# Product-key experts on one core: the order of the row gathers, top-k two heads ahead, and the sample on 128 partitions

## The reference

```
qry   = (h @ w_query) as 8 heads x 2 halves x 128
half  = qry . sub_keys                  # 8 heads x 2 halves x 128 scores
half_s, half_i = top_k(half, 16)        # per half
cand  = half_s[0] (+) half_s[1]         # 16 x 16 sums
best_s, best_j = top_k(cand, 16)        # 16 experts of a head
idx   = half_i[0] * 128 + half_i[1]     # at best_j
g     = softmax(best_s)
act   = gelu(h . expert_u[idx])         # 16 dot products per head
out  += (g * act) . expert_v[idx]       # 16 weighted rows per head
```

## Time and profile before

| | us |
|---|---|
| median of 3 runs (lowest, highest) | 1561.77 (1561.24, 1566.16) |
| span of the profiled execution | 1514.1 |

### The profile page before, as it was taken

The page is one execution under the profiler, slowest core; times in us unless marked ns, Lnnn a source line. Parts: engine busy times, 40 slices in busy tenths (PEclk is TensorE's granted clock), DMA queues, the critical chain, the costliest instruction groups (busy, mean ns, idle before and its releaser), DMA issues.

```text
span 1514.1 us, 12192 instructions
## 1 busy us (share of the span) xinstructions
PE 1087.7 (72%) x2877; PEld 468.7 (31%) x2877; DVE 807.6 (53%) x1626; ACT 204.8 (14%) x580; POOL 602.9 (40%) x586
## 2 busy tenths in 40 slices
PE   5997799638997986994576556856964775568456
PEld 1115454312332334852233222321122332223122
DVE  2000599963222575637555765558176557755651
ACT  0002010126001001121111111110101111112111
POOL 0000000442000000447766676665367666675761
PEclk9997899759997998997897778876568977788678
DMA  8675999746576245669999999898479989998893
GB/s 271 226 277 123 334 308 323 257 142 220 177 225 219 84 156 208 213 227 353 343 344 341 353 374 340 322 339 181 155 259 366 335 327 332 387 351 316 268 395 127
DMA packets 151174, 412.57 MB, mean 272 GB/s; under 512 B 14916, under 2 KB 21833, under 8 KB 151117
## 3 DMA queue, kind: packets, MB, share of 16 engines
q0 software_dynamic: 76288, 276.86, 51.2%
q1 hardware_dynamic: 60908, 113.78, 23.3%
q10 hardware_dynamic: 13938, 21.47, 4.2%
HBM read 405.87 MB, written 6.25 MB: 272 GB/s over the span
## 4 chain that ended last, share of the span: by engine, by line
PE 31%; issue 23%; DVE 16%; DMA 14%; POOL 11%; SPq 3%; ACT 2%; POOLq 1%; ACTq 1%; DVEq 0%; PEldq 0%
PE bank L517 17%; PE bank L514 12%; POOL ring L493 11%; DMA ring<-in_expert_u,idx 7%; DVE ra L1272 4%; DVE w L1276 4%; DMA rel_rows<-ra 2%; DMA ring<-in_w_ada 2%; DMA ring<-in_cache_k 2%; DVE ring L1580 2%; PE bank L525 1%; SPq L403 1%; SPq L402 1%; SPq L350 1%; DMA small<-in_rel_bias_table 1%
## 5 line engine op out<-in xcount | busy, mean ns | idle before, releaser
L517 PE MATMUL bank<-ring,mix 128*128 128x512 f32 (+1 forms) x1088 | 529.1, 651 | 295.5 <-ACT mix L1172 295.5
L1580 DVE CUSTOM_DVE_ANT_0 ring<-ring,r 128x1024 f32<-128x1024 f32 x256 | 312.2, 1225 | 240.6 <-DMA ring<-in_expert_u,idx 233.2
L517 PEld LDWEIGHTS bank<-ring,mix 128*128 128x128 f32 (+1 forms) x1088 | 213.5, 198 | 600.0 <-issue 359.7
L493 POOL DMA_INDIRECT ring<-in_expert_v,idx x272 | 271.5, 998 | 213.4 <-PE bank L517 145.2
L493 POOL DMA_INDIRECT ring<-in_expert_u,idx x272 | 286.9, 1055 | 130.0 <-issue 110.3
L1172 ACT ACTIVATE mix<-cst,small 128x128 f32<-128x128 f32 (+1 forms) x272 | 102.0, 393 | 343.7 <-PE bank L517 321.5
L514 PE MATMUL bank<-ht,ring 128*128 128x264 f32 x512 | 120.4, 397 | 2.4 <-PE bank L514 1.7
L517 PE MATMUL bank<-ring,lt 128*8 128x512 f32 x256 | 116.3, 608 | 2.4 <-DMA ring<-in_cache_v 1.6
L514 PE MATMUL bank<-ring,ht 128*128 128x512 f32 (+1 forms) x240 | 111.9, 616 | 2.5 <-ACT ht L1115 1.5
L514 PEld LDWEIGHTS bank<-ht,ring 128*128 128x128 f32 x512 | 99.5, 196 | 22.8 <-issue 5.7
L441 POOL TENSOR_TENSOR small<-small 128x1 f32<-128x1 f32 (+1 forms) x9 | 4.9, 549 | 252.7 <-DVE small L340 252.7
(11 more groups left out here) (297 smaller groups left out, 720.5 us busy)
## 6 DMA issues: line engine op xcount, KB each, us to landing
ring<-in_cache_k SPq DMA_DIRECT2D x128, 256.0 KB, 3.7
ring<-in_cache_v SPq DMA_DIRECT2D x128, 256.0 KB, 3.1
ring<-in_w_ada SPq DMA_DIRECT2D x12, 2048.0 KB, 7.9
ring<-in_w_in ACTq DMA_DIRECT2D x5, 2048.0 KB, 13.7
ring<-in_w_query SPq DMA_DIRECT2D x4, 2048.0 KB, 8.6
ring<-in_expert_u,idx POOLq DMA_INDIRECT x272, 6.3
ring<-in_expert_v,idx POOLq DMA_INDIRECT x272, 6.0
ring<-in_w_in SPq DMA_DIRECT2D x2, 2048.0 KB, 8.7
```

Source lines behind the costliest of these rows:

```text
L493: g.indirect_dma_start(ring_t[0:rows, col(s):col(s) + DM], None, table, bass.IndirectOffsetOnAxis(tok[0:rows, par * PK + k:par * PK + k + ...
L517: return nc.tensor.matmul(out, lhsT, rhs, start=False, stop=False, skip_group_check=True)
L1580: E.op(v.tensor_tensor_reduce(out=u, in0=u, in1=h2, scale=1.0, scalar=0.0, op0=ALU.mult, op1=ALU.add, accum_out=w[:, k:k + 1]), "u_slot_free")
```

## The change

- POOL: first the 16 U gathers of head 0; then for each step s the V gathers of head s and the U gathers of head s+1 in turn (one to one; around the sample in the ratio of their numbers).
- DVE: topk(0) and topk(1) ahead of head(0), then head(s), topk(s+2). tok has 4 places instead of 2. Scores, query copies and `best` (the softmax exponentials) follow this order: the first ones stand in the chunk loop of the query projection, the others inside the slot loops of PE and ACT (at slots 4 and 6).
- The sample as 128 partitions: the upper 64 take experts 0 to 7 of each (head, row) pair, the lower 64 experts 8 to 15. So 8 gathers of 128 rows for each table instead of 16 of 64 rows, 128x8 blocks on PE, and a copy of weights and query to the other half.
- Diagonals: 8 buffers instead of 4.
- All loops of the stage are written out, waits are on constants, and the `hold` increments of POOL and of topk are gone.
- finish(0) and finish(2) stand on DVE behind topk(11) in step 9 and topk(12) in step 10; on ACT behind diagonal 7 of these steps.

```diff
+DR = 8
+STEPS = 2 * PH + 1
+SAMPLE = PH
+IB = 4
+def slots_of(s):
+    return PK // 2 if s == SAMPLE else PK
+def first_of(s):
+    return sum(slots_of(i) for i in range(s))
...
 # POOL
-            def head(par, rows):
-                E.wait("idx_ready")
-                E.hold()
-                for name, table, col in (("u", eu, u_col), ("v", ev, v_col)):
-                    for k in range(PK):
...
-                        E.wait(name + "_slot_free")
-                        E.hold()
-                        s = k % UR
-                        g.indirect_dma_start(ring_t[0:rows, col(s):col(s) + DM], None, table, ...
+            def gather(name, table, col, s, k):
+                E.wait(name + "_slot_free")
+                n = first_of(s) + k
+                j = (s % IB) * PK + k
+                g.indirect_dma_start(ring_t[:, col(n % UR):col(n % UR) + DM], None, table, ...
+            E.wait("idx_ready")
+            for k in range(PK):
+                if k == UR // 2:
+                    q.wait_ge(sems("blocks_used"), 23)
+                gather("u", eu, u_col, 0, k)
+            for s in range(STEPS):
+                nv, nu = slots_of(s), slots_of(s + 1) if s + 1 < STEPS else 0
+                if nu:
+                    E.wait("idx_ready")
+                iv = iu = 0
+                while iv < nv or iu < nu:
+                    if iv * nu <= iu * nv and iv < nv or iu == nu:
+                        gather("v", ev, v_col, s, iv)
+                        iv += 1
+                    else:
+                        gather("u", eu, u_col, s + 1, iu)
+                        iu += 1
 # PE
-                if c == 2:
+                if c in (2, 5, 9):
                     scores()
...
+            for s in range(STEPS):
+                fb, rows = (4, 6, 2)[tile_of(s)], NB if s == SAMPLE else P
...
+                for k in range(slots_of(s)):
+                    if k == 6 and s + 3 < STEPS:
+                        scores()
+                    n = first_of(s) + k
+                    q.wait_ge(sems(f"v{n % UR}_in"), 16 * (n // UR + 1))
+                    E.wait("diag_w")
+                    for e in range(2):
+                        m = acc(bank[fb + e][0:rows, :], MIX[:, (n % DR) * P:(n % DR) * P + rows],
+                                ring_t[:, v_col(n % UR) + e * N:v_col(n % UR) + (e + 1) * N])
+                    E.op(m, "v_slot_free")
 # ACT
+            for s in range(STEPS):
+                E.wait("gelu_arg")
+                E.op(a.activation(wB, wB, ACT.Exp), "gelu_exp")
+                E.wait("w_ready")
...
+                for k in range(slots_of(s)):
+                    if k == 4 and s + 3 < STEPS:
+                        next_query(s + 3)
+                    n = first_of(s) + k
+                    E.wait("v_slot_free")
+                    E.op(a.activation(MIX[:, (n % DR) * P:(n % DR) * P + cols], src, ACT.Copy, ...), "diag_w")
+                    if k == 6 and s + 2 < STEPS:
+                        best(s + 2)
+                    if k == 7 and s in (SAMPLE + 1, SAMPLE + 2):
+                        finish(0 if s == SAMPLE + 1 else 2)
 # DVE
-                E.hold()          # seven of these in topk
...
+                if s == SAMPLE:
+                    up, dn = slice(0, AH * NB), slice(AH * NB, P)
+                    E.op(v.scalar_tensor_tensor(tok[up, at:at + 8], selk[up, 0:8], ...))
+                    step(v.scalar_tensor_tensor(tok[dn, at:at + 8], selk[dn, 8:PK], ...), "idx_ready")
...
-            topk(0, True)
-            for t in range(NT):
-                with E.loop(TRIPS[t], ...) as i:
-                    for e in range(2):
-                        head(e ^ t, P, H2[:, t, :], BASE[t] + 2 * e, i)
-                        topk(1 - (e ^ t))
-                if t == 0:
-                    head(0, AH * NB, RA[0:AH * NB, 5120:6144], 2 * PH)
-                    topk(1)
+            topk(0)
+            topk(1)
+            for s in range(STEPS):
+                head(s)
+                if s + 2 < STEPS:
+                    topk(s + 2)
+                if s == SAMPLE + 1:
                     finish(0)
-            finish(2)
-            head(1, P, H2[:, 1, :], BASE[1] + 4 * TRIPS[1])
-            topk(0)
-            head(0, P, H2[:, 1, :], BASE[1] + 4 * TRIPS[1] + 2)
+                if s == SAMPLE + 2:
+                    finish(2)
             finish(1)
```

More of the change, by code:

```diff
@@ L77, in constants @@
     head_sum = np.zeros((P, NB))
-    for p in range(AH * NB):
+    for p in range(P):
         head_sum[p, p % NB] = 1.0
@@ L110 @@
 C_REP = C_IOTA + PK
[L111 removed]
+C_SUM = C_REP + P
 C_OWN = C_SUM + 16
@@ L278, in build @@
         smst = small(12)
-        wS = [small(PK) for _ in range(2)]
+        wS = small(PK)
         wA, wB, wG = small(PK), small(PK), [small(PK) for _ in range(2)]
@@ L906, in _ @@
             E.tally(("made", "v_slot_free")).n = UR
[L907 to L914, removed]
+            for s in range(STEPS):
+                fb, rows = (4, 6, 2)[tile_of(s)], NB if s == SAMPLE else P
+                if s in (0, SAMPLE, SAMPLE + 1):
+                    for e in range(2):
+                        zero(bank[fb + e][0:rows, :], rows, MIX[0:NB, 2048:2560])
+                for k in range(slots_of(s)):
[3 more added lines that the diff above has]
+                    q.wait_ge(sems(f"v{n % UR}_in"), 16 * (n // UR + 1))
@@ L1154, in _ @@
             for e in range(2):
-                E.op(a.activation(RA[0:64, 5120 + e * N:5120 + (e + 1) * N], bank[1 + e][0:64, :], ACT.Copy),
+                E.op(a.activation(RA[:, 5120 + e * N:5120 + (e + 1) * N], bank[1 + e][:], ACT.Copy),
                      "h2r_out" if e else None)
[L1159 to L1164, removed]
-                E.wait("gelu_arg")
-                E.op(a.activation(wB[0:rows, :], wB[0:rows, :], ACT.Exp), "gelu_exp")
-                E.wait("w_ready")
-                out_rows = P if rows == P else NB
-                src = eye if rows == P else cst[0:rows, C_HS:C_HS + NB]
-                for k in range(PK):
-                    E.wait("v_slot_free")
-                    E.op(a.activation(MIX[0:rows, (k % 4) * P:(k % 4) * P + out_rows], src, ACT.Copy,
-                                      scale=wG[par][0:rows, k:k + 1]), "diag_w")
-                if nxt is not None:
-                    best(1 - par)
             def finish(t):
@@ L1594, in head @@
                 step(v.reciprocal(y, y))
-                E.wait("diag_w", PK)
-                E.op(v.tensor_tensor(wG[par][0:rows, :], x, y, ALU.mult), "w_ready")
+                if s >= 2:
+                    E.wait("diag_w", slots_of(s - 2))
+                E.op(v.tensor_tensor(wG[par][:, 0:n], x, y, ALU.mult), "w_ready")
             def finish(t):
```

137 lines of the change are left out of this document (48 added, 89 removed).

## The result

The changed kernel takes 1508.31 us (median of 4 runs, 1505.37 to 1522.65); the kernel before took 1561.51 us beside it (4 runs, 1559.03 to 1566.16). The ratio is 0.968, 95% interval 0.964 to 0.973: 3.2% faster, where 6.6% (1458 us) had been predicted.

What follows compares the result with a forecast made beforehand. Each step was taken as a V phase at PE's pace plus a U phase at POOL's. Head 1 at 703.6, steps 266.4 + 71.6 + 108 + 177.6 + 39.7, tail 42.9: span 1409.8, plus 47.7 gives 1458 us; range 1405 to 1520.

Steps and rivals of the forecast that it cites:

- top-k of head s+3, 718.93 + 0.17 - 709.34 = 9.8: On DVE, between a head's last dot product and the next head's first: top-k takes 9.8 us, from the earlier trace.
- fits by 1.1 us: First U slot free after 21.2 us, gather needing it due on POOL at 22.3 us, so 1.1 us to spare.
- the prediction's own sign of being wrong: Called wrong if POOL waits every step for U slots, PE slots stay at 3.4 us, or gathers stay at 1.24.
- The loss of 4.7 us by gathers beside dot products: POOL's gathers slow during DVE's back-to-back dot products after top-k: 4.7 us a step, making the step 44.4 us.
- 47.7 us lie around it: Difference between the profiled span of 1514.1 us and the timed median of 1561.77 us, kept unchanged in the forecast.
- The slow gathers of the earlier trace: On POOL behind each top-k: gathers of 1.98 us, 2.29 us apart, some five expected.
- Hold and straight-line code at 0: Fewer semaphore increments on POOL's gathers and unrolled loops' code fetches: each taken as 0 us.
- The sample at about 72 us: The two steps around the sample, now with 128-row gathers: 71.6 us together instead of 121.4.
- (1): Rival: PE loses its clock, V slots at 3.4 us, PE binds: 1563 or 1611 us; chance 0.06.
- (2): Rival: the transfers themselves bind at 357 GB/s, 47.0 us a step: 1493 us; chance 0.17.
- (4): Rival: alternation gains nothing in an ordinary step (queue heads blocking, code fetches), 48.6 us stays: 1519 us; chance 0.10.
- (3): Rival: POOL's slow gathers are covered, DMA at 411 GB/s binds, 41 us a step: 1409 us; chance 0.15.

Runs made afterwards that it cites:

- Experiment 4: Changed kernel with top-k cut into 14 dependent stages issued between the dot products of the head before, best exponent on ACT later: 1427.28 us, ratio 0.915.
- experiments 5: Kernel before plus five 1 MB blocks that nobody reads, loaded by SP when the weights of heads 1 to 14 are ready: 1604.67 us, one run.
- 6: Changed kernel with gathers of 128 rows of 1 KB instead of 4 KB, same POOL instructions: 1545.61 us, one run.
- 2: Changed kernel with the seven holds put back into top-k: 1522.94 us, ratio 0.978.
- Experiment 3: Changed kernel with only the gather order put back, all V of a head, then all U of the next: 1484.01 us, ratio 0.953.
- experiment 1: Kernel before run once more, no edit: span 1573.9 us at a time of 1575.69 us.
- experiment 9: Kernel of experiments 8 with the dot products of heads 2 to 7 reading the tokens from PSUM instead of SBUF: 1419.25 us, ratio 0.909.
- experiments 8: Kernel of Experiment 4 with a shorter DVE chain behind the last dot product of a head: 1417.48 us, ratio 0.909.
- kernel 7: Kernel of Experiment 4 with dot products over 512 instead of 1024 columns, all transfers kept: 1406.79 us, ratio 0.902.

## Why the prediction was wrong

**The step that failed** is "top-k of head s+3, 718.93 + 0.17 - 709.34 = 9.8". It measured 16.0 on average. The count around it held: if the U slot "fits by 1.1 us", whatever top-k takes above 9.8 + 1.1 = 10.9 us should come out as a wait of POOL, and it does, to within 0.6 us:

| step of head | top-k in it, us | above 10.9 | POOL's wait for the U slot | step |
|---|---|---|---|---|
| 1 to 2 | 21.3 | 10.4 | 10.5 | 55.0 |
| 2 to 3 | 11.7 | 0.8 | 0.3 | 45.8 |
| 3 to 4 | 21.4 | 10.5 | 10.4 | 55.5 |
| 4 to 5 | 11.5 | 0.6 | 0 | 47.1 |
| 5 to 6 | 13.8 | 2.9 | 3.1 | 49.4 |
| 6 to 7 | 10.7 | 0 | 0 | 47.0 |

So the prediction's own sign of being wrong came true, POOL waiting for U slots. The rival that should have stood there, top-k slower among gathers, was priced nowhere. The text took the durations of the earlier trace rows as fixed. They came from a place where POOL stood for PE between gathers, five in 9.8 us, and were moved to one where gathers follow each other every 1.24 us. Experiment 4 takes top-k's waits off that path and gets 81 us back; experiments 5 and 6 show that POOL's gathers are the cause, not the bytes; 2 and 3 rule out hold and straight-line code as the reason for the 1508 us.

**A second term was too small.** Steps whose top-k was in time took 45.8 to 47.1 us, not 44.4. The loss of 4.7 us by gathers beside dot products counted only one burst of slow gathers. Between 710 and 1460 a gather lasts 1.13 us on average, 0.19 more than the 0.94 that the prediction gave it outside the burst: about 6 us in a step of 32 gathers. Experiment 4, where POOL has no such waits, has steps of 46.8 us for the same reason.

**The base.** "47.7 us lie around it" is wrong; 1.8 do. The 1514.1 us of the profiled execution were not the timed 1562 less an overhead, but an execution in which the chain behind the last dot product took 2.3 us instead of 5.7 (experiment 1). It looks like the lateness that later met top-k; that it is the same was not shown. By the spans alone the forecast was 93.8 us short; adding 47.7 that don't exist hid half of it, and that 1508 still lies between 1405 and 1520 is in good part luck.

**What held.** The alternation at 1.24 us, and V no longer waiting at PE's pace. The slow gathers of the earlier trace rows: two to four of 1.9 to 2.0 us follow each top-k from head 3 on, and experiment 9 shows why. Hold and straight-line code at 0: gathers kept their gap of 0.30, and the fetches (23 packets on the queue of the earlier trace rows, 18 before) left no mark. The tail (42.2 against 42.9). The sample at about 72 us (79.2 and 72.6), though not all of the difference to 121.4 is the sample's own.

**The rivals.** (1) PE kept its clock in the main: the mean is 0.892, against 0.830 before. Slots of 3.4 us come singly after a pause (weight loads 0.85 us apart from 711.25 to 713.81, then 0.43). By the rule of the Trainium skill that the prediction cites here (TensorE: Matmul & The Clock Gate, section Loop structure matters more than you think), as the prediction reads it, the new order should have had the lower clock; the measurement went the other way. That rule speaks of long waits for DMA, and in this run PE waits 1.4 us on average for a V gather (174.4 us in 121 waits). (2) and (4) lie on either side of the result, at 1493 and 1519 us, but only with the 47.7 us: by the span, 1503.6, they are 58 and 33 us short. (2), transfers at 357 GB/s: the 375 of kernel 4 rise to 410 once POOL's gathers get shorter. (3) was out of reach, since POOL's own gathers last 1.13 us beside dot products. (4), a step that stays at 48.6: the step is even longer, 50.0 and 53.2. Its condition "heads of the queue blocking each other" did come about, as a U gather without a slot held up the V gathers behind it on POOL; that code fetches set the time is ruled out by experiments 3 and 6. What made the slot late, top-k, it doesn't name.

**What stays open.** Why a result is late in one place and not in the next, why lateness lasts up to 4 us after POOL's last gather, and why it spared the first execution. Gathers 1.24 us apart are not enough by themselves: in the changed kernel the gelu chain behind the last dot product runs beside such gathers and takes 2.2 to 2.5 us. Experiment 3 has gathers at PE's pace, as the kernel before has beside top-k, and yet a top-k of 11.8 us instead of 9.5; the holds are one difference between them that no run tested at this pace. POOL's own holds in front of the gathers were put back in no run; the late chain of experiment 1 ran with them. Head 1 is 7.1 us late: POOL waits 3.3 us for a U slot at 678, the rest was not traced. No experiment looked below "POOL's gathers in flight".

## What to carry to other kernels

A chain of short dependent DVE operations costs its profiled time only where it was profiled: before moving one beside a dense run of gathers from POOL, look how many gathers POOL issued beside it in the trace that gave its price, and how far apart. If they were fewer there, cut the chain into stages and issue them between long independent operations of the same engine, so that a late hand-over is covered. And set the span of the profiled execution against the timed runs before adding their difference as an overhead: it may be work that this execution was spared.

## What the runs showed of the hardware

- Beside POOL's gathers 1.24 us apart, what DVE hands on to its next dependent operation can come late, by up to 7.4 us at 408 GB/s and by up to 6.1 us with a quarter of the bytes (107 GB/s); 398 GB/s, mostly from SP's queue, delay it by nothing that shows (top-k 9.5 us). Not every chain is met: gelu's in the changed kernel is not.
- Among DVE's dot products a gather lasts 1.08 to 1.19 us on average with both operands in SBUF, 0.95 to 0.96 us with one in PSUM (experiments 8 and 9); the dot product itself lasts 1.22 and 1.21 us.
- A DMA share of 1.01 is no proof of a full path: 375 GB/s at 1.01 in kernel 4, 410 at 1.02 in kernel 7, with the same transfers.
